# VectorE's order within a slot of the pair steps: low part of o, mean squares and normalised tokens ahead of the slot's logits

## What is computed

```
h = rms_norm(x, g_norm1) * (1 + scale1) + shift1
qa, ka, va, qb, kb, vb, qi, ki, wi, logf, ga, gb = split(h @ w_in)
qa, ka, qb, kb = rms_norm per head of 64, with gains
per block of 128 queries:
    scores = sum_h relu(qi . ki) * wi, masked;  sel = top_k(scores, 128)
    oa = softmax(qa . ka[sel] / 8 - slope * dist) . va[sel]
    ob = softmax(qb . kb / 8 + F_q - F_k, masked) . vb
merged = sigmoid(ga) * (oa @ w_o_a) + sigmoid(gb) * (ob @ w_o_b)
x = x + gate1 * (merged @ w_out)
x = x + gate2 * (relu(h2 @ w_up)**2 @ w_down)
```

## Time and profile before

| | us |
|---|---|
| median of 3 runs | 978.58 (977.5 to 979.12) |
| the profiled execution | 978.89 |
| its span, first to last instruction | 977.1 |
| TensorE busy in the span | 940.6 (96%) |
| VectorE busy | 489.6 (50%) |
| ScalarE busy | 393.0 (40%) |
| POOL busy | 139.6 (14%) |
| mean granted clock of TensorE | 0.982 |

### The profile page before, as it was taken

The page is one execution under the profiler, slowest core; times in us unless marked ns, Lnnn a source line. Parts: engine busy times, 40 slices in busy tenths (PEclk is TensorE's granted clock), DMA queues, the critical chain, the costliest instruction groups (busy, mean ns, idle before and its releaser), DMA issues.

```text
span 977.1 us, 19815 instructions
## 1 busy us (share of the span) xinstructions
PE 940.6 (96%) x7546; PEld 861.4 (88%) x7546; DVE 489.6 (50%) x1154; ACT 393.0 (40%) x813; POOL 139.6 (14%) x139
## 2 busy tenths in 40 slices
PE   8889989899999989999999998999999999999998
PEld 7588668778788878998899998999999999999997
DVE  2553767864635686841157547454333244542232
ACT  3254655654566766433223224433211134431221
POOL 4100232141234575300000000000000000000000
PEclk9789999999999999999899999999999999999999
DMA  9536673354423564777323330323322333223212
GB/s 317 199 104 181 183 256 115 114 163 128 140 71 92 170 211 144 237 218 238 107 65 91 105 87 23 109 86 94 100 86 86 90 101 89 86 87 104 89 44 88
DMA packets 176233, 124.54 MB, mean 127 GB/s; under 512 B 14739, under 2 KB 152019, under 8 KB 176164
## 3 DMA queue, kind: packets, MB, share of 16 engines
q1 hardware_dynamic: 176034, 123.50, 41.5%
q10 hardware_dynamic: 130, 0.10, 0.0%
HBM read 116.99 MB, written 6.59 MB: 126 GB/s over the span
## 4 chain that ended last, share of the span: by engine, by line
PE 71%; issue 19%; DVE 7%; ACT 2%; POOL 1%; POOLq 0%; ACTq 0%; DVEq 0%
PE bank L952 19%; PE bank L953 18%; PE bank L954 18%; PE bank L1033 2%; PE bank L1056 2%; PE bank L1012 2%; PE bank L1042 2%; PE bank L859 1%; PE bank L1074 1%; PE bank L881 1%; PE bank L1087 1%; PE bank L1018 1%; PE bank L1097 1%; DVE sel L1881 1%; DVE ms L1926 0%
## 5 line engine op out<-in xcount | busy, mean ns | idle before, releaser
L952 PE MATMUL bank<-h_hi,w_hi 128*128 128x260 f32 x1360 | 397.3, 292 | 9.8 <-DVE h_lo L1765 6.5
L953 PE MATMUL bank<-h_lo,w_hi 128*128 128x260 f32 x1360 | 388.1, 285 | 0.0
L954 PE MATMUL bank<-h_hi,w_lo 128*128 128x260 f32 x1360 | 387.7, 285 | 0.0
L952 PEld LDWEIGHTS bank<-h_hi,w_hi 128*128 128x128 f32 x1360 | 259.8, 191 | 32.5 <-issue 24.4
L953 PEld LDWEIGHTS bank<-h_lo,w_hi 128*128 128x128 f32 x1360 | 260.1, 191 | 0.0
L954 PEld LDWEIGHTS bank<-h_hi,w_lo 128*128 128x128 f32 x1360 | 259.9, 191 | 0.0
L952 PE MATMUL bank<-u_hi,w_hi 128*128 128x260 f32 x512 | 145.2, 284 | 0.0
L953 PE MATMUL bank<-u_lo,w_hi 128*128 128x260 f32 x512 | 144.8, 283 | 0.0
L954 PE MATMUL bank<-u_hi,w_lo 128*128 128x260 f32 x512 | 144.8, 283 | 0.0
L2222 DVE TENSOR_TENSOR w_lo<-raw,w_hi 128x1024 fp32r<-128x1024 f32 x62 | 76.0, 1226 | 135.1 <-ACT w_hi L1641 135.1
L1641 ACT ACTIVATE w_hi<-raw 128x1024 fp32r<-128x1024 f32 x62 | 65.4, 1055 | 140.3 <-PE bank L954 140.3
(11 more groups left out here) (316 smaller groups left out, 1178.1 us busy)
## 6 DMA issues: line engine op xcount, KB each, us to landing
raw<-in_w_in SPq DMA_DIRECT2D x44, 512.0 KB, 4.1
part<-in_w_ada SPq DMA_DIRECT2D x32, 512.0 KB, 5.6
raw<-in_w_up SPq DMA_DIRECT2D x32, 512.0 KB, 4.1
raw<-in_w_down SPq DMA_DIRECT2D x32, 512.0 KB, 4.1
ada<-in_w_ada SPq DMA_DIRECT2D x4, 2048.0 KB, 13.6
kv<-in_cache_k_b SPq DMA_DIRECT2D x16, 256.0 KB, 4.3
qbc<-q_d SPq DMA_DIRECT2D x16, 256.0 KB, 5.0
kv<-in_cache_k_a SPq DMA_DIRECT2D x16, 256.0 KB, 4.3
```

The costliest lines, as they stand in the source:

```text
L952: mm(out, hi[:, k, :], x_h, start=first and k == ks[0], stop=False)
L953: mm(out, hi[:, k, :], x_l, start=False, stop=False)
L954: end = mm(out, lo[:, k, :], x_h, start=False, stop=last and k == ks[-1])
```

## The change

In VectorE's list for a slot, `rest_o`, `mean_squares` and `normalize` stand ahead of `logits`, with `rest_o` first. The other engines' lists are the same, and so is every instruction.

```diff
@@ -2075,15 +2075,15 @@
                     dve.wait_ge(masks_made, 2 * p)
                 if 0 <= U - 1 < N_UNITS:
                     inverse_sum(U - 1)
-                if 0 <= U < N_UNITS:
-                    logits(U)
+                if s == 4 and p >= 2:
+                    rest_o(p - 2)
                 if p < N_PAIRS:
                     if s in (2, 4):
                         mean_squares(p, s // 2 - 1)
                     if s in (3, 5):
                         normalize(p, s // 2 - 1)
-                if s == 4 and p >= 2:
-                    rest_o(p - 2)
+                if 0 <= U < N_UNITS:
+                    logits(U)
                 if 0 <= U < 2 * TOPK_P // 8:
                     top_round(U)
                 if s == K_BACK and p < N_PAIRS:
```

## The result

The changed kernel took 965.71 us (median of four executions, 964.87 to 966.26) beside 978.04 us (975.78 to 979.12) for the kernel before: ratio 0.9876, 95% interval 0.9856 to 0.9896, 12.3 us less. Compared again later, with more executions, it was 967.50 us beside 976.23 us: ratio 0.9918 (0.9894 to 0.9942), 8.7 us less. The forecast was 9.1 us less, 969.5 us. The profiled execution took 965.95 us, its span is 964.2 us.

What follows compares the result with a forecast made beforehand. TensorE, busy 940.6 of 977.1 us, was taken as the bound. Pair gains 2.4 + 1.5 + 1.7 + 1.7 + 0.6 + 0.6 + 0.6 = 9.1 us off 978.58 gave 969.5 us, range 965.8 to 974.0.

Steps and rivals of the forecast that it cites:

- Bound and waits: TensorE bounds; its waits for `o_lo` (L1056) and `tok` (L1087) can go, at most 11.5 us.
- Pair 1: L1087 wait shrinks from 1.91 to about 0.2 us, and the clock drop after it goes: 2.4 us won.
- a cap by `w_lo`: Pair 1: POOL's `w_lo` waits for VectorE's `fdiag`, limiting TensorE's lead to at most 1.7 + 0.8 us.
- Pair 2: 2.5 us of waits go, but VectorE runs unbroken to `fdiag`; 1 us is given back, 1.5 won.
- Pairs 3 to 6: L1056 and L1087 waits in pairs 3 and 4 go, 1.7 us each; pairs 5 and 6 win 0.6 each.
- other drops of the clock: Anywhere the shifted work meets them: about 1 us, counted in the forecast's spread.
- Pair 7: Scaling stretched by POOL's `w_lo` stands ahead of logits; 0.6 of 2.7 us of waits won.
- without the lock: Pair 7, if VectorE and POOL did not share an exclusive port lock: about 1.9 us won, time 968.2 us.
- Everything goes: Rival: all 11.5 us plus about 1 us of clock, nothing given back in pairs 2 and 7: 966.1 us; chance 0.12.
- Only `o_lo`: Rival: `tok` stays bound by POOL's power, only the 5.1 to 5.5 us at L1056 go: 973.3 us; chance 0.11.
- Slower: Rival: later logits pass through ScalarE's exps to TensorE, 21.6 us against 11.5 won: 988.7 us; chance 0.06.
- the waits of rows 3: TensorE's L1087 and L1056 waits placed by pair; no other engine's result was said to stand close behind them.

Runs made afterwards that it cites:

- only `o_lo` moved: Changed kernel with mean squares and normalised tokens put back behind logits, so only the low part of o stands ahead: ratio 0.9977 to the kernel before.
- two rounds less: Changed kernel without two of VectorE's top-k rounds in pair 2 and their picks: ratio 0.9865 to the kernel before, pair steps 359.63 us.
- the split ones: Kernel before and changed kernel, each with the 32 products at L1119 halved over slots 6 and 7 of pair 3: ratios 0.999 and 0.9867 to the kernel before.

## Why the prediction was right

The time was 8.7 to 12.3 us less where 9.1 was forecast, and the pair steps show 8.3 to 9.7. The first comparison alone, 965.71 us, lies 0.1 us below the stated range of 965.8 to 974.0; it holds the 4.6 us from outside the pair steps. The second lies inside. By pair, in the first two traces, from pair 1's turn of q on (the lead that after gained up to the same turn of the next pair, us):

| pair | forecast | measured |
|---|---|---|
| 1 | 2.4 | 2.75 |
| 2 | 1.5 | 1.56 |
| 3 | 1.7 | 0.37 (1.83 up to the turn of k, then -1.46) |
| 4 | 1.7 | 1.87 |
| 5 | 0.6 | 0.62 |
| 6 | 0.6 | 0.68 |
| 7 and behind | 0.6 | 0.91 |
| sum | 9.1 | 8.76 |

The sum came so close partly by luck. The forecast counted about 0.7 us of clock in pair 1 (2.4, less 1.7 of wait); measured over the pair steps the clock gave nothing, since either kernel stood 6.8 us at the lower level. Without the clock, 8.4 was forecast and 8.8 measured.

**Bound and waits.** Right. The waits that went are those named, no new wait for logits of the odd slots came up, and POOL's power is in time in pairs 1 to 4.

**Pair 1.** Right, with one thing more. The wait went (1.91 to 0.16), and the drop of the clock near 147 us was not there: 1.75 of wait and, by the price that the experiments gave, 1.5 of clock. That the drop went because the wait went is not shown: it came in three of the four traces with the long wait and in none of the ten with a short one, but "only `o_lo` moved" kept the wait and had no drop. I had counted on a cap by `w_lo`; what took 0.54 us back was TensorE's turn at L1114, waiting for `k_fm`. That copy stood on ScalarE behind exps that waited for VectorE's logits, and VectorE had no gap there, so VectorE is already the bound in pair 1, a place that the prediction gave to pair 2 alone. ScalarE's rows in the changed kernel:

```profile
146.47 0.72 ACT L1452 ACTIVATE lg<-lg,stat 128x512 f32<-128x512 f32 x1 [0.48 <-DVE stat L1918]
...
147.19 0.57 ACT L1483 ACTIVATE k_fm<-bank 128x512 f32<-128x512 f32 x1
```

**Pair 2.** The amount was right, and the reason: VectorE runs without a break up to `fdiag`. These rows of VectorE, POOL and TensorE in the changed kernel are the ones to read with the earlier trace rows:

```profile
188.18 1.29 DVE L2072 TENSOR_TENSOR fdiag<-fbc,cmask 128x512 f32<-128x512 f32 x2
```

```profile
189.55 2.36 POOL L813 TENSOR_TENSOR w_lo<-raw,w_hi 128x1024 fp32r<-128x1024 f32 x1 [15.57 <-DVE fdiag L2072]
```

```profile
192.01 0.36 PE L952 MATMUL bank<-h_hi,w_hi 128*128 128x260 f32 x1
```

`w_lo` ends at 191.91 and TensorE starts on it at 192.01, as before. The place was half wrong: I expected one wait of about 1.5 us in the turn after pair 2. There are 0.81 us there, 0.63 of which before had too, and 0.58 us at L1114. The row of before:

```profile
197.13 0.33 PE L1042 MATMUL bank<-ident,lg 128*128 128x128 f32 x1 [0.63 <-ACT lg L1458]
```

**Pairs 3 to 6.** Right to within 0.2 us, but for the clock. *This is the term that was mis-sized*: "other drops of the clock, which can fall on other work once everything shifts (about 1 us, the price of this one)". It stood in the spread and not in the sum. The drop at L1119 was in the trace of before, 3.4 us long; in the new order it is 6.8 us in every trace that has the 32 products in one piece, except with two rounds less (3.4 us), and costs 1.5 us more. The drop that was missing in pair 1 gave the same back. Without the drop at L1119 in either kernel, the split ones, the change wins 297.52 - 286.09 = 11.43 us from pair 1 on, of which 1.03 is the lost race behind pair 7 and about 1.5 the drop in pair 1.

**Pair 7.** Right as to what happens: the scaling stood until `w_lo` ended, ahead of logits, and 1.92 us of wait is left at L1087 where 1.5 or more was named. It stood 2.09 us and not 1.02, since VectorE came to it sooner. With the scaling left out, the lead from pair 7's turn of q on is 2.13 us, where the prediction named about 1.9 without the lock. The Trainium skill ("SBUF — State Buffer", section on who interferes with whom) says that the order of issue decides who blocks, and that a VectorE instruction with two SBUF inputs contends with POOL's reads too. The traces agree on both: scaling at 0.17 us when 0.03 us ahead of `w_lo`, at 2.09 behind it; key gain at 0.69 ahead of POOL's product, 2.76 behind it. The prediction drew on this page only for the scaling; the second rule decided about 1 us behind pair 7 in two of the three traces of the old order.

**The rivals.** "Everything goes" fell on pairs 2 and 7, which gave back what was forecast. "Only `o_lo`" fell: the tokens' work pays, and `o_lo` moved by itself is worth 2.7 us. "Slower" did not happen, but its mechanism is there in small, against the reading that no other engine's result stands close behind the waits of rows 3: the late logits that ScalarE's exps pass on reach TensorE in pairs 1 and 2, with 0.54 and 0.58 us at L1114 and 0.18 us more than before at L1042, 1.3 us in all where it needed over 11.5.

What stays open: what sets the moment at which the clock falls at L1119, with which its length goes, and whether the change moved it or chance did, with two traces of each kernel; what brings the drop in pair 1; and why most of the 4.6 us outside the pair steps was won. The kernel before varies there by as much from one execution to the next, which makes the change an unlikely cause, but that part was traced to one only as far as the early drop goes.

## What to carry to other kernels

When the bounding engine waits for a helper engine, look at what the helper did just before: if the wanted result's inputs were ready and it did something wanted two slots later, reorder its list, and move the whole chain (squares, power, tokens), since moving one link only takes the wait to the next. Then look for what the new order runs into: another engine's long instruction beside which this one stands still, a queue that now starts later, a stretch of short products behind which the clock falls. The version worth keeping here is the change with the 32 short products split over two slots, 963.08 us (0.9867 of before). Its 2.7 us over the change are read from the pair steps; the two kernels were not timed against each other.

## What the runs showed of the hardware

- The granted clock fell to the 1.2 GHz level at 32 products of 8 columns (256 ns each as listed, 3.7 us in a row at full clock) with TensorE listed as busy all the time, in all ten traces that have them in one piece, and in none of the four where they were split in two times 16. A stretch at the lower level within the pair steps was 3.4 or 6.8 us long in every trace, and 3.4 us of it cost 1.5 us of this work.
- VectorE's scaling (128x8, 0.17 us) stood until POOL's subtraction (128x1024) ended when it started behind it, 0.70 to 2.12 us, and kept its 0.17 us when it started 0.03 us ahead. VectorE's key gain (two inputs in SBUF) and POOL's product held each other up whichever started first: 0.69 and 2.92 us, or 2.71 to 2.91 and 2.37 to 2.38. Hundredths of a microsecond decide, and with them up to 1 us of the whole.
- TensorE's pace at full clock lay at one of two levels in these traces, and executions of one kernel fell on either. In windows from 650 to 950 us, late in the span, the first and the second trace of before show 2496 and 2517 matmuls:

```profile
650.00:950.00 300.00, 300.00 (x2496) 300.00 (x2495) 115.29 (x203) 85.47 (x147) 0.00 (x0) 1.00 0.30 88
```

```profile
650.00:950.00 300.00, 300.00 (x2517) 299.96 (x2516) 114.28 (x200) 84.68 (x144) 0.00 (x0) 1.00 0.31 89
```

That is 0.8%, 2.5 us in this window alone, over a quarter of what the change is worth. The two traces of after show 2499 and 2518, and all 14 traces lie at 2496 to 2499 or at 2517 and 2518, with both levels on chips 7 and 11. In the pair steps it does not show: the two traces of after, one at each level, agree there to 0.01 us. It is a reason to compare stages and not only spans.
